# Gate and up products by column group, the first expert's rows chosen on chip, and a table of row numbers laid out by slot row

## The reference

```python
t = rmsnorm(x2, ffn_norm)                      # 768 x 1024
gl = t @ router_group + router_group_bias      # 4 groups: the best one
el = t @ router_expert + router_expert_bias    # 32 experts: the best 2 inside that group
gates = p_group * renormalised p_expert        # 2 experts for each token
for e in range(32):                            # w_gate, w_up: 1024 x 256; w_down: 256 x 1024
    y = (silu(t @ w_gate[e]) * (t @ w_up[e])) @ w_down[e]
    out = out + gates[:, e:e + 1] * y
return rmsnorm(x2 + out, final_norm)
```

## Time and profile before

| | |
|---|---|
| median of 3 runs | 808.14 us (805.69 to 811.24) |
| the profiled execution | 808.41 us |
| its span in the trace | 806.6 us |
| mean granted clock of TensorE | 0.977 |
| PE busy | 741.6 us (92% of the span) |
| PEld, DVE, ACT, POOL busy | 412.6, 316.5, 213.9, 201.8 us |
| moved by DMA | 154.64 MB, mean 192 GB/s |

### The profile page before, as it was taken

The page is one execution under the profiler, slowest core; times in us unless marked ns, Lnnn a source line. Parts: engine busy times, 40 slices in busy tenths (PEclk is TensorE's granted clock), DMA queues, the critical chain, the costliest instruction groups (busy, mean ns, idle before and its releaser), DMA issues. The chain is left out here.

```text
span 806.6 us, 12402 instructions
## 1 busy us (share of the span) xinstructions
PE 741.6 (92%) x4028; PEld 412.6 (51%) x4029; DVE 316.5 (39%) x900; ACT 213.9 (27%) x575; POOL 201.8 (25%) x478
## 2 busy tenths in 40 slices
PE   6899999999988999998999973999998999999895
PEld 3455544444455666664455552555554555555542
DVE  3853121100088988881545562111121112111136
ACT  2433210011176776772211110111110111111123
POOL 1224232220024230232001123441332434442110
PEclk9999999999999999999999986999998999999998
DMA  8703002000050000000792158899999999999957
GB/s 301 298 1 105 0 1 104 1 0 1 18 196 0 2 2 1 1 2 0 295 423 118 57 207 309 280 343 373 373 339 392 387 358 354 395 364 384 387 188 308
DMA packets 36728, 154.64 MB, mean 192 GB/s; under 512 B 9642, under 2 KB 10794, under 8 KB 23744
## 3 DMA queue, kind: packets, MB, share of 16 engines
q1 hardware_dynamic: 29024, 138.20, 45.5%
q0 software_dynamic: 7648, 15.75, 5.8%
HBM read 142.29 MB, written 20.03 MB: 201 GB/s over the span
## 5 line engine op out<-in xcount | busy, mean ns | idle before, releaser
L1442 PE MATMUL banks<-arena 128*128 128x512 f32 (+1 forms) x384 | 163.3, 579 | 9.4 <-DMA arena<-w_in 7.5
L1707 PE MATMUL banks<-arena 128*64 128x256 f32 x1280 | 156.6, 396 | 6.8 <-DMA arena<-w_up 2.7
L1707 PEld LDWEIGHTS banks<-arena 128*64 128x64 f32 x1280 | 94.9, 137 | 60.7 <-issue 12.9
L1442 PEld LDWEIGHTS banks<-arena 128*128 128x128 f32 x384 | 72.1, 193 | 84.8 <-issue 77.7
L1598 PE MATMUL banks<-arena 128*128 128x512 f32 x192 | 86.4, 598 | 1.1 <-DVE arena L1189 1.1
L1716 PE MATMUL banks<-arena 128*64 128x512 f32 x320 | 79.8, 610 | 0.5 <-ACT arena L1004 0.5
L1353 DVE TENSOR_TENSOR arena<-arena,banks 128x128 f32<-128x128 f32 x40 | 11.5, 288 | 166.0 <-ACT arena L996 145.6
L1145 DVE TENSOR_REDUCE arena<-banks 128x1 f32<-128x512 f32 (+1 forms) x96 | 55.2, 599 | 49.3 <-PE banks L1514 41.9
L927 ACT ACTIVATE arena<-banks,arena 128x512 f32<-128x512 f32 (+1 forms) x96 | 58.3, 612 | 43.3 <-DVE arena L1148 20.7
L1598 PEld LDWEIGHTS banks<-arena 128*128 128x128 f32 x192 | 35.1, 190 | 38.8 <-issue 37.5
L996 ACT ACTIVATE arena<-banks 128x128 f32<-128x128 f32 x40 | 11.1, 278 | 160.3 <-PE banks L1707 160.3
(11 more groups left out here) (191 smaller groups left out, 886.0 us busy)
## 6 DMA issues: line engine op xcount, KB each, us to landing
arena<-w_gate SPq DMA_DIRECT2D x32, 1024.0 KB, 6.3
arena<-w_up SPq DMA_DIRECT2D x32, 1024.0 KB, 10.1
arena<-w_down SPq DMA_DIRECT2D x32, 1024.0 KB, 12.5
arena<-w_in SPq DMA_DIRECT2D x3, 2048.0 KB, 8.3
arena<-pair_rows SPq DMA_DIRECT2D x5, 1024.0 KB, 11.2
arena<-w_out SPq DMA_DIRECT2D x1, 4096.0 KB, 12.8
arena<-xT SPq DMA_DIRECT2D x6, 512.0 KB, 10.2
arena<-x SPq DMA_DIRECT2D x6, 512.0 KB, 10.6
```

What stands on the lines that cost most here:

```text
L1442: last = nc.tensor.matmul(bank(mm % 2)[:, 0:GROUP_COLS[g]], xgT[:, t, c, :], w[:, c, :], start=(c == 0), stop=(c == DC - 1))
L1707: last = nc.tensor.matmul(bank(b)[h * SLOTS:(h + 1) * SLOTS, 0:2 * P].rearrange("p (g n) -> p g n", g=2), x_eT[i][:, c, :], w[:, :, c, h, ...
```

## The change

Three edits, in the words of the code:

1. **Column groups.** PE column group 0 now takes all 256 gate columns and group 1 all 256 up columns, each read without a step. So gate lies in PSUM partitions 0 to 63 and up in 64 to 127. Silu and product are 64x256 instead of 128x128, and h needs two transposes of 64 rows instead of one of 128.
2. **The first block's rows are chosen on chip.** `h2` is stored without the gain, by ACT instead of DVE; the gain is multiplied in where DVE takes a row transpose out of PSUM. For expert 0, DVE makes for each tile a matrix (128x64) that is the norm's factor where a token of this tile belongs to a slot of expert 0 (`choose`), and PE multiplies it with x2 over all six tiles; ACT copies the 64 rows out and PE transposes them. No gather for expert 0. DVE's counts come after expert 0's rows, and PE's wait for them after expert 0's `gate_up`. The down product of expert 0 comes ahead of `gate_up` of expert 1.
3. **The table.** The scatter writes three ready numbers (12 bytes), at an address by slot row, so that the load is 64 runs of 4.2 KB for each half of the partitions, 128 in all, instead of 1408 of 128 bytes. DVE needs three more small instructions in `slots` and `ids_further` is gone. The load is issued by ACT behind its first silu, and POOL waits for it only before the first further block. SP's queue loses the wait and the loads; in it the store of tile 5's residual moves ahead of experts 4 and 5, and expert 31 waits for `chosen_psum`.

```diff
-            sp.dma_start(gain_ffn, A["ffn_norm"].to_broadcast([P, D])).then_inc(gffn_in, 16)
...
             sp.wait_ge(oproj, 2 * NT)
+            store_residual(NT - 1)
             load_expert(0, 4)
             load_expert(0, 5)
-            store_residual(NT - 1)
-            sp.wait_ge(ids_scattered, 2 * NT * 16)
-            for h in range(2):
-                sp.dma_start(yids_sb[h * SLOTS:(h + 1) * SLOTS, NE:].rearrange("r (b e) -> r b e", e=NE),
-                             ids_dram.rearrange("(b r e) o -> r b (e o)", b=NBLK, e=NE)[:, 1:, :]).then_inc(ids_loaded, 16)
             sp.wait_ge(x2_stored, NT * 16)
...
+            sp.wait_ge(chosen_psum, 1)
             load_expert(NGRP - 1, members(NGRP - 1)[-1])
...
                     with pool.If(n > 0):
+                        await_count(ids_loaded, 32)
                         await_count(e_xeT_psum, before + 1)
...
-            gather_main(0, 0)
+            pool.sem_inc(id_ready, 1)
             gather_main(0, 1)
             note_pairs(NT - 1)
...
             pool.wait_ge(counts_ready, 1)
-            pool.wait_ge(ids_ready, 3)
+            pool.wait_ge(ids_ready, 2)
...
+            def ffn_norm(t):
+
+                act.wait_ge(norm_ready, t + 1)
+                if t >= 2:
+                    act.wait_ge(h2_stored[t % 2], 16 * (t // 2))
+                act.activation(h2[t % 2].rearrange("n (c p) -> n c p", c=DC), x_tok[:, t, :].rearrange("n (p c) -> n c p", c=DC),
+                               ACT.Copy, scale=rs[:, t:t + 1]).then_inc(h2_ready, 1)
+
...
+            act.wait_ge(chosen_psum, 1)
+            act.activation(x_sel, bank(4), ACT.Copy).then_inc(chosen_rows, 1)
             act.wait_ge(gates_in, 1)
...
-                act.activation(silu_t, bank(1)[:, 0:P], ACT.Silu).then_inc(silu_done, 1)
+                act.activation(silu_t, bank(1)[0:SLOTS, 0:FF], ACT.Silu).then_inc(silu_done, 1)
...
+            def load_further_ids():
+
+                act.wait_ge(ids_scattered, 2 * NT * 16)
+                for h in range(2):
+                    act.dma_start(ids_sb[h * SLOTS:(h + 1) * SLOTS, 3 * NE:3 * NBLK * NE - h],
+                                  ids_dram.rearrange("(r n) o -> r (n o)", r=SLOTS)[:, 3 * NE + h:]).then_inc(ids_loaded, 16)
...
-            def ffn_norm(t):
+            def norm(t):
                 dve.wait_ge(rms2_ready, t + 1)
-                link(dve.reciprocal(rs[:, t:t + 1], rs[:, t:t + 1]))
...
-                dve.scalar_tensor_tensor(h2[t % 2].rearrange("n (c p) -> n c p", c=DC),
-                                         x_tok[:, t, :].rearrange("n (p c) -> n c p", c=DC), rs[:, t:t + 1],
-                                         gain_ffn.rearrange("n (p c) -> n c p", c=DC), ALU.mult, ALU.mult).then_inc(h2_ready, 1)
+                dve.reciprocal(rs[:, t:t + 1], rs[:, t:t + 1]).then_inc(norm_ready, 1)
+                dve.wait_ge(norm_ready, t + 1)
...
+            def choose(t):
+
+                for i, mask in enumerate((m1_all, m2_all)):
+                    dve.tensor_scalar(share[:, i:i + 1], mask[:, t, 0:1], rs[:, t:t + 1], None, ALU.mult).then_inc(dve_chain, 1)
+                    chain[0] += 1
+                dve.wait_ge(dve_chain, chain[0])
+                dve.wait_ge(onehot_ready, 2 * t + 2)
+                link(dve.tensor_scalar(select[:, t, :], onehot[:, 0, 0:SLOTS], share[:, 0:1], None, ALU.mult))
+                dve.scalar_tensor_tensor(select[:, t, :], onehot[:, 1, 0:SLOTS], share[:, 1:2], select[:, t, :],
+                                         ALU.mult, ALU.add).then_inc(select_ready, 1)
+
...
             slots(NT - 1)
+            dve.wait_ge(xeT_psum, 1)
+            dve.tensor_tensor(x_eT[0], bank(0).rearrange("p (c n) -> p c n", c=DC), gain_eT, ALU.mult).then_inc(xeT_ready, 1)
 
             dve.wait_ge(counts_psum, 1)
...
-                dve.tensor_tensor(h_tok, silu_t, bank(1)[:, P:2 * P], ALU.mult).then_inc(h_ready, 1)
+                dve.tensor_tensor(h_tok, silu_t, bank(1)[SLOTS:P, 0:FF], ALU.mult).then_inc(h_ready, 1)
...
+            def choose(t):
+
+                pe.wait_ge(select_ready, t + 1)
+                for h in range(2):
+                    last = nc.tensor.matmul(bank(4)[h * SLOTS:(h + 1) * SLOTS, :], select[:, t, :],
+                                            x_tok[:, t, h * 512:(h + 1) * 512], start=(t == 0), stop=(t == NT - 1))
+                return last
+
...
             router(NT - 1, 1)
+            for t in range(3):
+                choose(t)
             rank(NT - 1)
-            counts = bank(1)[:, 0:NE]
+            choose(3)
+            place(NT - 1)
+            choose(4)
+            choose(5).then_inc(chosen_psum, 1)
+            counts = bank(2)[:, 0:NE]
...
-                w = w[:, 0:4096].rearrange("p (g c n h) -> p g c h n", g=2, c=DC, h=2)
+                w = w[:, 0:4096].rearrange("p (g c n) -> p g c n", g=2, c=DC)
                 for c in range(DC):
-                    for h in range(2):
-                        last = nc.tensor.matmul(bank(b)[h * SLOTS:(h + 1) * SLOTS, 0:2 * P].rearrange("p (g n) -> p g n", g=2),
-                                                x_eT[i][:, c, :], w[:, :, c, h, :],
+                    for g in range(2):
+                        last = nc.tensor.matmul(bank(b)[g * SLOTS:(g + 1) * SLOTS, 0:FF], x_eT[i][:, c, :], w[:, g, c, :],
                                                 start=(c == 0), stop=(c == DC - 1))
...
-                pe.wait_ge(h_ready, k + 1)
-                nc.tensor.transpose(bank(3)[:, 0:P], h_tok, ident).then_inc(hT_psum, 1)
+                await_count(h_ready, k + 1)
+                h_row = h_tok.rearrange("n (p j) -> n j p", j=2)
+                for j in range(2):
+                    last = nc.tensor.transpose(bank(3)[:, j * SLOTS:(j + 1) * SLOTS], h_row[:, j, :], ident[0:SLOTS, 0:SLOTS])
+                last.then_inc(hT_psum, 1)
...
+                    early = first and s == 1
...
+                    if early:
+                        down_weights(g, 0)
+                        down_before(k, g, 0, last_done)
                     pe.wait_ge(xeT_ready, e + 1)
                     gate_up(1, s % 2, weights(g, s)).then_inc(gu_done, 1)
                     if not isinstance(g, int) or e + 1 < NE:
                         transpose_rows(g, s + 1)
-                    if not isinstance(g, int) or e:
+                    if first and s == 0:
+                        pe.wait_ge(counts_ready, 1)
...
+                    elif not early:
                         down_weights(g, s - 1)
...
-            pe.wait_ge(rows_in[0], 16)
-            rows_transpose(0, 0, range(DC)).then_inc(xeT_psum, 1)
-            pe.wait_ge(counts_ready, 1)
+            pe.wait_ge(chosen_rows, 1)
+            x_sel_c = x_sel.rearrange("n (p c) -> n c p", c=DC)
+            for c in range(DC):
+                for h in range(2):
+                    half = slice(h * SLOTS, (h + 1) * SLOTS)
+                    last = nc.tensor.matmul(bank(0)[half, c * SLOTS:(c + 1) * SLOTS], x_sel_c[half, c, :], ident[half, half],
+                                            start=True, stop=True)
+            last.then_inc(xeT_psum, 1)
```

More of the change, by code:

```diff
@@ L244, in build @@
         nw_pool = k.take(3 * 8)
-        ids_main = k.take(NE).bitcast(u32)
         id_cur = k.take(RING + 1).bitcast(u32)
@@ L1288, in _ @@
                 x2T_evac(t)
-                ffn_norm(t)
+                norm(t)
                 route(t)
@@ L1753, in pe_group @@
             def pe_group(g):
-                words = load_counts(pe, g)
+                first = isinstance(g, int) and g == 0
+                if not first:
+                    words = load_counts(pe, g)
                 for s in members(g):
                     e = g * RING + s
-                    n, before = extras(words, s)
-                    k = e + before
                     if is_last(g, s):
```

130 lines of the change are left out of this document (72 added, 58 removed).

## The result

The changed kernel takes 815.8 us, the median of six runs (814.9 to 817.4), and the kernel before 807.9 in the same series. The ratio is 1.0103, with a 95% interval of 1.008 to 1.0126. The forecast was 803.0 us, with a range of 797 to 808: it missed by 12.8 us, and on the wrong side of no change.

The account below looks back on a forecast made before the run. PE was taken to bound the expert stage up to expert 15's down product, then the DMA stream. 6.7 us gained at the start less 1.7 in further blocks gave 5.0: 808.41 to 803.4, median 803, range 797 to 808.

Parts of the forecast that it names:

- One chain with a change of hands: Expert stage: PE sets the pace to expert 15's down product, then the DMA stream of ten experts until 758 us.
- if nothing else is late: Condition on the expert-stage chain: what moves its first part, where PE sets the pace, moves the end.
- cost and gain nothing: The table's load, POOL's wait and the extra `slots` instructions: all behind work not waited for, so zero.
- `gate_up` of expert 0 at 488.0: Start of the expert stage, rows chosen on PE: `gate_up` 8.6 us sooner, counted at 3.8 us.
- Rows of expert 1 at 494.6: Gather through DRAM, moving only with the store of `h2`: rows usable 7.9 us after the gather; 1 us sooner if ACT's norm takes 1.0.
- `gate_up` of expert 1 at 498.3, of expert 2 at 503.8: PE at the start of the expert stage: 5.7 us sooner at expert 1, 6.7 us sooner at expert 2.
- Rival 3: The start gains less: 1.2 GHz through choosing and `gate_up` of expert 0, start gains 4.5, total 805.5 us; chance 0.16.
- DMA can't become the bound earlier than before: Weight stream after the restart: DMA leads by 12 us and PE by 6.7, so DMA binds no earlier.
- rival 1: DMA sets all of it: its restart 12 us earlier would all arrive, 796 us; chance 0.17, together with dense `gate_up` reading gaining.
- the forecast's 6.7 us: Gain at the start, counted at `gate_up` of expert 2: 503.8 against 510.51.
- The column groups: Each block: dense reading gains 0.02 us, silu 0.10 and product 0.13 more, second transpose zero (-0.1 to +0.26).
- Rival 2: The pair of transposes eats the gain: 0.26 us more a block gives 809 us, deciding from 0.23; chance 0.15.

Follow-up runs that it names:

- fit_late31: after_shift101 with the three transfers of expert 31's weights issued only when expert 1's rows have landed; 808.6 us, ratio 1.0012.
- after_fit_warm: after_shift101 with 17 idle products on PE between `gate_up` of expert 0 and the wait for expert 1's rows; 812.0 us, ratio 1.0046.
- before_columns: The kernel before with the column groups alone (dense `gate_up`, 64 x 256 silu and product, two transposes of h); 807.8 us, ratio 1.0000.
- after_shift101: The changed kernel with idle increments put into POOL's program, so that its loop of unchanged length lies from 760 to 1129; 807.5 us, ratio 0.9992.
- fit_cut: after_shift101 with the table of further rows loaded only for blocks 2 to 4 of 12, 147 KB instead of 528; 805.6 us, ratio 0.9979.
- fit_cut_start: fit_cut with the counts loaded ahead of the wait for expert 1's rows and 4 idle products in that wait; 804.9 us, ratio 0.9984.

## Why the prediction was wrong, point by point

- *"One chain with a change of hands", which holds "if nothing else is late", and the table at "cost and gain nothing".* This is the step that failed most, for 8.3 us. The prediction went through the waits of PE, DVE, ACT, SP and DMA; the six waits and the arithmetic that the table adds to POOL's loop are in none of its terms. What the runs showed in their place is two turns of that loop at 9.0 and 9.3 us instead of 2.9, and rows that come late behind them. Nor did it ask what POOL's 2.86 us of "issue" at each turn is, and what it would be with a longer body. Late is not hidden there: the gather of expert 13's first further block is issued at 597.61, and PE needs its rows at about 601.7.
- *`gate_up` of expert 0 at 488.0.* Right: 488.74, at 2.4 GHz; 0.84 us of these times is that the whole execution lay later (router at 475.09 instead of 474.25). Choosing took 0.93 us for each tile (forecast 0.94), the 32 small products 2.14 (2.6), and ACT's norm 2.16 (2.0).
- *Rows of expert 1 at 494.6.* They came at 496.54, 1.1 us late beside the 0.84. POOL's copy came at 487.62 instead of 486.68, nearly all of it that same shift, and from its start to the rows it took 8.9 us instead of 7.9. Taking expert 31's weights out of the way didn't bring the rows clearly sooner (fit_late31).
- *`gate_up` of expert 1 at 498.3, of expert 2 at 503.8.* 502.81 and 508.79. Beside the 1.9 us of the rows two terms were missing: 1.1 us in which PE loads the counts between the row transposes and h, and the clock. Rival 3 had the clock low through the choosing and `gate_up` of expert 0. In the changed kernel's trace it was at its full level in both and fell in the wait for the rows that the prediction had itself written down; in 7 of the 11 traces with the whole change it was low in `gate_up` of expert 0 as well, as the rival had it. Down of expert 0 took 3.68 us instead of 1.9, and `gate_up` of expert 1 4.24 instead of 3.8.
- *"DMA can't become the bound earlier than before", and the 12 us of lead.* This failed too. The restart 12 us sooner filled gaps that were not 12 us long: the DMA share in the kernel before was 0.86 from 480 to 500 us and 0.83 from 500 to 520, 6.2 us of idle time together. Some of it went to the table. With PE 3.7 us sooner the end stayed where it was. So with POOL's loop repaired rival 1's mechanism holds for the end, with a far smaller size than its 12 us. By this the forecast's 6.7 us, had PE started so soon, would not have arrived; no run has that start. PE still counts when it is late: in after_fit_warm 4.5 of 7.4 us arrived.
- *"The table costs nothing."* On the side of DMA this failed too, by a small amount: 2.2 us of all DMA engines, now in a stretch where they are never idle. A second load cost 3 to 4 us; what the first costs is 1 to 2 us by the cut, which the intervals don't secure. In the kernel before a cut of its own table brought nothing (808.3 for 807.5 us).
- *The column groups.* The sum was right and two terms of it were not. Reading the columns side by side gives 0.17 us a block (forecast 0.02; the prediction had two reasons for nothing, the spacing in its rows and the sentence on a step of 2 words, and the measurement decides against both). The pair of transposes costs 0.12 (forecast 0, bounds -0.1 and +0.26). Expert 8 with its further block takes 13.02 us instead of 13.01 (from its `gate_up` to that of expert 9). Less an ordinary block that is 6.53 for 6.47. Rival 2, which needed 0.23 us more a block, is out: before_columns has 0.05 less.
- *1.7 us for the further blocks.* Too much by itself: at 0.06 us each the seven make 0.4 us, since what silu and the product cost more is mostly given back by the faster `gate_up`.

The three errors (POOL's code, the table, the start) all point the same way. Without the first the kernel comes out at 807.5 (after_shift101), inside the range of 797 to 808, but as no change and not as the 803 that I gave; that it lies inside is no merit of the sum, since the terms of the start, the table and the further blocks were wrong.

What stays open: why the way of expert 1's rows is 1 us longer than that of expert 0's was; how much of the last 4.5 us is the table and how much the rest of the weight stream; and whether the block rule (three in a row of 128 instructions) holds for other engines. It was inferred from six places of one loop and then tested with two, which have the same beginning.

No version beats the kernel before by more than its interval. fit_cut (805.6 us, 0.9958 to 1.0001) and fit_cut_start (804.9 us, 0.9955 to 1.0014) come nearest; both leave out part of the table, which would have to be loaded under a condition.

## What to carry to other kernels

Before adding instructions to a loop that an engine runs from its instruction buffer, look at the "issue" gap at its turn and at the instruction packets in that stretch: here a lone packet went with a body that was held, and then a few instructions more, or code put in ahead of it on that engine, cost microseconds at every turn. Moving an earlier start through a chain of two resources needs both counted: write down how long the second one was idle, not only how much sooner it restarts. A transfer that costs nothing in an idle stretch can have a price once the change fills that stretch.

## What the runs showed of the hardware

A turn of POOL's loop took 2.9 us with 1 instruction packet of 8192 bytes in 138 us, and 6 to 10 us with 10 or 11. The place alone decided: the same body of 369 instructions turned in 2.9 us at place 760 and in 9.1 and 6.2 at 779. A record of a 128 x 512 product with 128 columns of weights took 0.44 us (14.86 us for 34), where down's, in two column groups of 64, took 0.23 (1.87 for 8). `gate_up` took 3.84 us where it read every second word and 3.67 us where it read the words side by side, for the same 32 records.
